# State space stage of a two-layer trunk: the way back from state layout to channel layout goes through TensorE instead of through DMA

## What is computed

```
ys = lax.map(run_block, (u, ...))          # y = d*u + both scan directions, per group of 16 channels
y = jnp.moveaxis(ys, 0, 2).reshape(B, L, D)
z = jax.nn.gelu(y).astype(h.dtype) @ w_glu
a, g = jnp.split(z, 2, axis=-1)
return a * jax.nn.sigmoid(g)
```

## Time and profile before

| | us |
|---|---|
| median of 3 executions | 2883.32 |
| lowest and highest of them | 2877.65 and 2887.63 |
| the profiled execution | 2880.59 |
| its span, first to last instruction | 2878.5 |

### The profile page before, as it was taken

The page is one execution under the profiler, slowest core; times in us unless marked ns, Lnnn a source line. Parts: engine busy times, 40 slices in busy tenths (PEclk is TensorE's granted clock), DMA queues, the critical chain, the costliest instruction groups (busy, mean ns, idle before and its releaser), DMA issues.

```text
span 2878.5 us, 43282 instructions
## 1 busy us (share of the span) xinstructions
PE 2623.6 (91%) x17226; PEld 2112.1 (73%) x17226; DVE 1885.4 (66%) x1930; ACT 1102.3 (38%) x881; POOL 135.4 (5%) x200
## 2 busy tenths in 40 slices
PE   6989999977698999999999967769889999999997
PEld 2348888723487888888888851658778888888886
DVE  6876666678456776767777739556676666555554
ACT  4453333444333333334444340133333333444442
POOL 1020000000001000000000032100020000000000
PEclk9999999987899999999999969889999999999998
DMA  8988888622353887877878759378747777555551
GB/s 252 340 307 296 283 268 282 219 75 88 103 173 106 287 285 259 284 271 276 283 262 285 264 164 234 102 237 283 255 145 234 233 237 233 184 187 180 190 189 45
DMA packets 257452, 639.00 MB, mean 222 GB/s; under 512 B 45442, under 2 KB 46468, under 8 KB 252740
## 3 DMA queue, kind: packets, MB, share of 16 engines
q1 hardware_dynamic: 238420, 580.55, 60.9%
q0 software_dynamic: 11008, 35.99, 4.3%
q10 hardware_dynamic: 7920, 21.01, 2.0%
HBM read 613.50 MB, written 19.79 MB: 220 GB/s over the span
## 4 chain that ended last, share of the span: by engine, by line
PE 82%; DVE 11%; ACT 2%; DMA 2%; issue 1%; SPq 1%; ACTq 1%; DVEq 0%
PE PS L271 47%; PE PS L275 23%; PE PS L224 3%; DVE Pb L1808 2%; DVE acc L1803 1%; PE PS L934 1%; PE PS L734 1%; PE PS L755 1%; ACT Pb L988 1%; DMA araw<-in_ada_w 1%; PE PS L188 1%; DVE wlo L261 1%; PE PS L465 1%; PE PS L667 1%; ACTq L429 1%
## 5 line engine op out<-in xcount | busy, mean ns | idle before, releaser
L271 PE MATMUL PS<-H,whi 128*128 128x512 f32 x5888 | 1865.1, 398 | 83.2 <-DVE wlo L261 59.7
L275 PEld LDWEIGHTS PS<-H,wlo 128*128 128x128 f32 x5888 | 1113.7, 189 | 262.7
L261 DVE TENSOR_TENSOR wlo<-raw,whi 128x2048 fp32r<-128x2048 f32 x368 | 843.9, 2294 | 705.4 <-ACT whi L257 704.3
L257 ACT ACTIVATE whi<-raw 128x2048 fp32r<-128x2048 f32 x368 | 705.1, 1917 | 1231.4 <-PE PS L271 1190.6
L275 PE MATMUL PS<-H,wlo 128*128 128x256 f32 x5888 | 1162.6, 279 | 0.0
L271 PEld LDWEIGHTS PS<-H,whi 128*128 128x128 f32 x5888 | 904.8, 190 | 88.7 <-DVE wlo L261 66.5
L180 DVE SCALAR_TENSOR_TENSOR acc<-araw,cact,acc 128x1024 f32<-128x1024 f32 x240 | 307.9, 1283 | 2.0 <-DMA araw<-in_ada_w 1.5
L988 ACT ACTIVATE Pb<-PS 128x1024 f32 (+5 forms) x117 | 118.0, 1034 | 135.4 <-PE PS L667 52.1
L988 ACT ACTIVATE H<-Pb 128x512 fp32r (+3 forms) x138 | 90.5, 657 | 36.7 <-DVE Pb L1444 22.8
L1492 DVE TENSOR_TENSOR H<-Pb,H 128x512 fp32r<-128x512 f32 x128 | 87.6, 684 | 0.0
L1911 POOL TENSOR_SCALAR X<-X,small 128x256 f32<-128x256 f32 x64 | 64.6, 1022 | 437.7 <-DVE Pb L1444 427.8
(11 more groups left out here) (266 smaller groups left out, 1366.8 us busy)
## 6 DMA issues: line engine op xcount, KB each, us to landing
raw<-in_mlp_w SPq DMA_DIRECT2D x256, 1024.0 KB, 6.2
araw<-in_ada_w SPq DMA_DIRECT2D x274, 512.0 KB, 4.7
raw<-in_mix_w_in SPq DMA_DIRECT2D x64, 1024.0 KB, 7.8
raw<-in_s_w_glu SPq DMA_DIRECT2D x32, 1024.0 KB, 7.5
acc<-in_ada_w SPq DMA_DIRECT2D x40, 512.0 KB, 8.2
raw<-in_ada_w POOLq DMA_DIRECT2D x32, 512.0 KB, 4.0
raw<-in_mix_w_out SPq DMA_DIRECT2D x16, 1024.0 KB, 5.1
vmat<-Pb ACTq DMA_DIRECT2D x8, 1024.0 KB, 7.5
```

The source lines that it names most:

```text
L257: nc.scalar.activation(whi[:, s % 2, :], raw[:, s, :], ACT.Copy).then_inc(S("hi_done"), 1)
L261: nc.vector.tensor_tensor(wlo[:, s % 2, :], raw[:, s, :], whi[:, s % 2, :].bitcast(F), ALU.subtract).then_inc(S("lo_done"), 1)
L271: return nc.tensor.matmul(PS[:, b, :], w, H2[:, :, k, :], start=first, stop=last, skip_group_check=True)
L275: return nc.tensor.matmul(PS[:, b, 0:T], w, H2[:, 0, k, :], start=False, stop=last, skip_group_check=True)
```

## The change

The 64 transfers of `channels_back` are gone from SP, ACT and POOL. PE brings the channels back instead. `PERM` is the identity with its rows in the order of the state layout, loaded by SP in eight small transfers. For each quarter PE multiplies `YT` by 32 of its columns at a time: the output is 32 partitions of PSUM, the sum runs over all 128 partitions, and 128 columns move. That is 32 matmuls for a quarter, 128 in all, into banks 2q and 2q+1. ACT rounds `Hhi` straight from PSUM (`back_hi`), DVE subtracts from PSUM (`back_low`). Since blocks of the GLU write banks 0 to 3 first, PE waits for `h_ready` 14, the first two quarters' `Hlo`.

`IM` moves from the columns of `whi` to those of `wlo`, so that `whi` is free during the gelu. SP loads slabs 0 and 1 of the GLU at `mat_used` 14 and slabs 2 and 3 at 16. ACT cuts the high halves of slabs 0 and 1 after the third quarter's sigmoid, DVE the low half of slab 0 ahead of the last `gelu_in` and that of slab 1 between the second and third `back_low`. A matmul by zeros (2 columns) after `within(3)` tells DVE by `im_used` that `IM` has been read.

```diff
-    IM = WF[:, 0:4096].rearrange("p (t m) -> p t m", t=64)
+    IM = WF[:, 4096:8192].rearrange("p (t m) -> p t m", t=64)
-    GLF = WF[:, 4096:8192]
-    GF = GLF.rearrange("p (k j n) -> p k j n", k=16, j=4)
+    PERM = acc[:, 1776:1904]
...
-                    channels_back(sp, 0, 0, 2)
+                    sp.wait_ge(S(f"{SCALE2.name}_freed"), 1)
+                    for g in range(2):
+                        for j in range(4):
+                            load(PERM[64 * g + 16 * j:64 * g + 16 * j + 16],
+                                 a["ident"][32 * j + 16 * g:32 * j + 16 * g + 16], "ld_perm")
+                    first = plan_glu[0]
+                    sp.wait_ge(S("mat_used"), 14)
+                    slab_loads(sp, 0, first.B, first.G, first.src, slabs=range(2))
                     sp.wait_ge(S("mat_used"), 16)
-                    first = plan_glu[0]
-                    slab_loads(sp, 0, first.B, first.G, first.src)
-                    channels_back(sp, 1, 0, 3)
+                    slab_loads(sp, 0, first.B, first.G, first.src, slabs=range(2, 4))
...
+                def channels_back(q):
+
+                    pe.wait_ge(S("ge_in"), 3 if q < 2 else 4)
+                    pe.wait_ge(S("y_ready"), q + 1)
+                    for k in range(2):
+                        ks = slice(4 * q + 2 * k, 4 * q + 2 * k + 2)
+                        for j in range(4):
+                            for a_ in range(4):
+                                last = nc.tensor.matmul(
+                                    PS[32 * a_:32 * a_ + 32, 2 * q + k, :].rearrange(
+                                        "p (k j n) -> p k j n", k=2, j=4)[:, :, j],
+                                    PERM[:, 32 * j:32 * j + 32],
+                                    YT.rearrange("p (k a) n -> p a k n", a=4)[:, a_, ks], start=True, stop=True)
+                    last.then_inc(S("y_back"), 1)
...
+                        if q == 3:
+                            nc.tensor.matmul(PS[0:64, 4, 0:2], ones[:, 0:64], ZERO2, start=False, stop=False,
+                                             skip_group_check=True).then_inc(S("im_used"), 1)
                     across(q)
+                pe.wait_ge(S("ld_perm"), 128)
+                for q in range(4):
+                    channels_back(q)
+                pe.wait_ge(S("h_ready"), 14)
...
+                def back_hi(g):
+                    act.wait_ge(S("y_back"), g + 1)
+                    run(Hhi[:, 4 * g:4 * g + 4, :].rearrange("p k t -> p (k t)"), bank(2 * g, 2), sem="o_hi")
...
+                    if q == 3:
+                        back_hi(0)
                     act.wait_ge(S("ge_cube"), q + 1)
                     run(GET[q % 2], GET[q % 2], ACT.Sigmoid, "ge_sig", scale=2 * GELU_C * 0.044715)
-                channels_back(act, 1, 1, 3)
...
+                    if q == 2:
+                        for sl in range(2):
+                            split_hi(act, 0, plan_glu[0].B, plan_glu[0].G, sl)
+                for g in range(1, 4):
+                    back_hi(g)
...
-                    blocks(plan_glu)
+                    blocks(plan_glu, early=2)
...
+                    def back_low(g):
+
+                        v.wait_ge(S("o_hi"), 3 + g)
+                        gs = slice(4 * g, 4 * g + 4)
+                        tt(Hlo[:, gs].rearrange("p k t -> p (k t)"), bank(2 * g, 2),
+                           Hhi[:, gs].rearrange("p k t -> p (k t)").bitcast(F), ALU.subtract
+                           ).then_inc(S("h_ready"), 1)
...
                     for q in range(4):
+                        if q == 3:
+                            v.wait_ge(S("im_used"), 1)
+                            split_lo(v, 0, plan_glu[0].B, plan_glu[0].G, 0)
                         gelu_in(q)
                         if q:
                             gelu_out(q - 1)
                         gelu_cube(q)
                     gelu_out(3)
+                    for g in range(2):
+                        back_low(g)
+                    split_lo(v, 0, plan_glu[0].B, plan_glu[0].G, 1)
+                    for g in range(2, 4):
+                        back_low(g)
...
-            channels_back(pool, 0, 1, 2, "g_soft")
-            channels_back(pool, 1, 2, 3, "g_soft")
```

More of the change, by code:

```diff
@@ L430, in spread @@
                         HS[32 * a_ + 16 * g:32 * a_ + 16 * g + 16, ks, j, :]).then_inc(S(f"{landed}{half}"), 16)
-    def channels_back(q, half, share, shares, landed="g_ready"):
-        q.wait_ge(S("y_ready"), 2 * half + 2)
-        ks = slice(8 * half, 8 * half + 8)
-        for i in range(share, 32, shares):
-            g, j, a_ = i // 16, i // 4 % 4, i % 4
-            q.dma_start(GF[32 * a_ + 16 * g:32 * a_ + 16 * g + 16, ks, j, :],
-                        YT[64 * g + 16 * j:64 * g + 16 * j + 16].rearrange("p (k a) n -> p a k n", a=4)[
-                            :, a_, ks]).then_inc(S(f"{landed}{half}"), 16)
     def shift_part(pe, c):
@@ L1224, in s5_act @@
                     run(GET[q % 2], HF[:, 1024 * q:1024 * (q + 1)], ACT.Square, "ge_sq")
+                    if q == 3:
+                        back_hi(0)
                     act.wait_ge(S("ge_cube"), q + 1)
                     run(GET[q % 2], GET[q % 2], ACT.Sigmoid, "ge_sig", scale=2 * GELU_C * 0.044715)
-                channels_back(act, 1, 1, 3)
-                for g in range(4):
-                    act.wait_ge(S(f"g_ready{g // 2}"), 352 if g // 2 else 256)
-                    act.wait_ge(S(f"g_soft{g // 2}"), 160 if g // 2 else 256)
-                    run(Hhi[:, 4 * g:4 * g + 4, :].rearrange("p k t -> p (k t)"), GLF[:, 1024 * g:1024 * (g + 1)],
-                        sem="o_hi")
+                    if q == 2:
[3 more added lines that the diff above has]
+                    back_hi(g)
             first = plan_in[0]
@@ L1843, in _ @@
                     link(tt(mod, SHIFT_SUM.rearrange("p (x r) -> p x r", x=4), bias, ALU.add))
-                    for g in range(4):
-                        v.wait_ge(S("o_hi"), 3 + g)
-                        gs = slice(4 * g, 4 * g + 4)
-                        tt(Hlo[:, gs].rearrange("p k t -> p (k t)"), GLF[:, 1024 * g:1024 * (g + 1)],
-                           Hhi[:, gs].rearrange("p k t -> p (k t)").bitcast(F), ALU.subtract
-                           ).then_inc(S("h_ready"), 1)
                     v.wait_ge(S("h_ready"), 16)
-                    prev = split_lows(plan_glu)
+                    prev = split_lows(plan_glu, early=2)
                     add_block(*prev, 1)
```

## The result

| | before | after |
|---|---|---|
| median, us | 2880.59 (2877.65 to 2887.63, 4 executions) | 2853.98 (2848.43 to 2859.09, 4 executions) |
| the profiled execution | 2880.59 | 2854.89 |
| its span | 2878.5 | 2853.1 |

The ratio is 0.991, with a 95% interval of 0.9892 to 0.9927: 26.6 us faster by the medians, 21 to 31 by the interval.

What follows compares the result with a forecast made beforehand. PE bounds the GLU, which waits behind the state space stage for transfers and halves. An earlier start of 21.2 us plus 2.0 of clock, 23.2, gave 2857.4 from the profiled execution, 2860 against the median; range 2852 to 2869.

Steps and rivals of the forecast that it cites:

- What bounds the kernel: At the GLU: PE bounds it, so bringing its start forward brings its end forward as much, if slabs keep up.
- Start of the GLU: Behind the state space stage: PE starts the GLU at 1873.2 instead of 1894.4, released by DVE, 21.2 us gained.
- The tiny matmul: Matmul by zeros ahead of across(3): costs 0.4 us, taken between 0 and 0.6.
- A quarter of the return: PE's permutation matmuls, 64 records a quarter: 32.5 ns each, 2.1 us a quarter.
- The value from L830: Nearest profiled row, same form with 32 moving columns: 8.1 ns a record, giving 32.5 ns for 128 columns.
- the lower bound of 1.7: Permutation quarter with four tiles fully side by side: 27 ns a record, 1.7 us a quarter.
- The rival with one tile after another: Permutation at 108 ns a record: GLU starts at 1890.5, gain 5.9 us, time 2877; chance 0.08.
- The 135 ns: Permutation record if no weight load is hidden, by the skill's rule: GLU start 1897.5, about 2884, no gain.
- Slabs late, gelu held up: Early halves ahead of last square and gelu_in: late slabs cost 1.4 us (2861.4) or 4.8 us (2865); chance 0.12.
- the cover: DVE's low half of slab 0 ends 0.3 us ahead of gelu_in(3), so the early operations cost nothing.
- The clock: GLU's first slab: 2.0 us lost to clock 0.50 saved; rival of clock falling in the pause, 2863.9, chance 0.20.
- Block 1 starved: Next GLU block's first slab landing after 16.4 us comes 6 us late, 2866; chance 0.06.

Runs made afterwards that it cites:

- the second set: No edit: the changed kernel and the kernel before run again; 2856.08 us against 2878.51, ratio 0.9924.
- the second traces: Profiles of the unedited changed kernel and kernel before, each traced again; from third gelu_in to the GLU 22.3 us and 42.5 us.
- one_tile: Changed kernel with every matmul of the return writing the first 32-wide tile, other channels left out; GLU starts 40.2 us after the third gelu_in.
- late_loads: Changed kernel with loads of slabs 0 and 1 moved back to mat_used 16, cuts still early; GLU starts 32.1 us after the third gelu_in.
- late_all: Changed kernel with both loads and cuts of slabs 0 and 1 late, leaving only the return through TensorE; 2860.18 us, ratio 0.9946 against before.
- no_tiny: Changed kernel without the matmul by zeros, the last matmul of within(3) signalling instead; GLU starts 22.7 us after the third gelu_in.
- reorder_no_tiny: Changed kernel without the matmul by zeros, DVE doing gelu_out(2) before slab 0's low half and back_low(0) before gelu_out(3); 2855.22 us, ratio 0.9918 against before.
- perm_twice: Changed kernel with each quarter's matmuls of the return issued twice; GLU starts 30.0 us after the third gelu_in.
- late_cuts: Changed kernel with slabs 0 and 1 loaded early but cut only behind the halves of H; GLU starts 27.2 us after the third gelu_in.

## Why the prediction was right, point by point

The forecast was 2860 us, 23.2 us less than before, in a range of 2852 to 2869. Measured were 2854, 26.6 less, and 22.4 less in the second set.

- **What bounds the kernel: right.** What brought the GLU's start forward arrived at the norm behind it (23.95 of gain at the start, 25.7 at the norm, the difference being the clock in the first slab).
- **Start of the GLU: right mechanism, 1.6 us short.** Forecast 21.2, measured 19.6, and 20.2 between the second traces. Of the 1.6 that are missing, 0.9 is the hole in `across(3)`, which no term of mine held, 0.4 that PE began 0.47 us behind DVE's second low half and not 0.1, and 0.3 that the fourth `gelu_in` came later than hole and tiny matmul explain. It was DVE that released PE, as forecast.
- **The tiny matmul: right.** 0.4 forecast, 0.4 measured with the hole left out.
- **A quarter of the return: 2.1 forecast, 1.9 measured.** The value from L830 was as near as the lower bound of 1.7. (Of the 123 records in that row two belong to L465, which changes little.) The rival with one tile after another was wrong for this order, and one_tile shows what it would have cost: its price of 108 ns was right, and so was its effect, 17 us (40.2 against 23.3) where my sum gives 17.3. The rule of the Trainium skill, TensorE: Matmul & The Clock Gate, Part 3, that weight loads overlap matmuls in flight only when the row group differs, fails here: L942's tiles all have 128 rows, and a record takes 29 ns with its weight load, and 110 when the tile stays the same, which is the price that I had taken for a matmul without its load. The 135 ns that I had estimated from that page came up nowhere.
- **Slabs late, gelu held up: did not happen, right as a mechanism.** The low half of slab 0 ended 10.7 us after the third `gelu_in`, exactly as forecast. I gave the cover 0.3 us, and it was 2.0 in the first trace and 1.0 in the second, since `gelu_in(3)` came later: by the tiny matmul, whose 0.4 us I had left out of the cover, by 0.3 without a known cause, and in the first trace by the hole. Slab 1 landed late enough for ACT to wait 1.36 us for it, which held up nothing. late_loads shows the mechanism: 10 us.
- **The clock: right in kind, 0.3 too much.** 2.0 forecast, 1.7 measured, since a first slab at full clock takes 5.9 us and not 5.6. The pause of 1.83 us did not bring the clock down; in late_all, with 5.36, it fell.
- **Block 1 starved: did not happen.** ACT's cuts went on in steps of 5.57 us from the first slab.
- **Not in the forecast at all:** the 4.3 us ahead of the stage. By the profiled pair they are why the first set came out beyond the forecast, 2.6 of them by the clock in a stretch that is the same in both kernels. The stage and the clock together gave 21.3 us (21.9 between the second traces' norms), a little less than forecast. That the first total of 26.6 lies above 23.2 and not below it is luck; what the change itself gave lies 1.3 to 1.9 us below.

## What to carry to other kernels

Moving data between partitions by 64 small transfers cost 16 us more here than a permutation on an idle TensorE. Half of the transfers stood behind the last result, while three of the four quarters of matmuls ran beside the gelu. Matmuls with 32 output partitions should change tile from one to the next: 29 ns a record in turn, 61 in blocks of four, 110 in one tile. An early conversion of the next weights is worth its time only if its load comes early as well; else it stands in the engines' order ahead of work that was ready.

## What the runs showed of the hardware that I had not expected

**Holes in PE's stream at fixed places.** In `across(3)` PE paused for 0.2 to 0.9 us after record 164 of 256 in eight of nine traces with slab loads beside it, waiting for nothing that the profile shows, and in late_all and late_loads, without such loads, it did not. In no_tiny and reorder_no_tiny, where the two records of the tiny matmul ahead of it are gone, 90 records follow the hole instead of 92: it is fixed in the stream of instructions, not in time. In perm_twice the next hole comes 255 records later (92 + 163), each a matmul and a weight load, and in reorder_no_tiny there is one of 0.97 us 254 records later (90 + 164). But the last hole of perm_twice, 2.50 us, comes only 127 records behind the one before it. The page counts the transfers of the instruction queue:

```profile
q8 instruction: 75, 1.23, 0.2%
```

That is 16 KB each. That these are PE's next instructions, fetched late when slabs fill the DMA engines, fits all of this and is argued, not shown; the second set's trace of the changed kernel had the loads and no hole. late_loads has a hole in `across(2)`, after record 102 of 256, and no other trace has one there. The last 1 MB matrix loads were under way ahead of it, and no slabs:

```profile
1842.59 5.75 PE L927 MATMUL PS<-Pb,raw 64*64 64x64 f32 x154 [1.21 <-issue]
```

It lies 384 records ahead of the usual place (154 + 64 + 2 + 164). All the distances, 127, 254, 255 and 384, are near multiples of 128; one of 255 alone does not fit them.

**The clock.** It held 1.00 through pauses of 1.83 and, in perm_twice, 2.50 us, and was at 0.50 behind pauses of 5.36 us (late_all, late_cuts) and 10.51 us (late_loads).
